# Two layers of attention and retention on one core: the last head's steps spread among the attention branch's groups, and a product's operands made by halves

## What is computed

```python
h = rms_norm(x, norm_g[layer])
z = h @ w_in[layer]
qa, ka, va, ga, qr, kr, vr, gr, gm = split_columns(z)
# attention branch: 8 query heads, 2 key heads, head dimension 64
oa = block_attention(qa, ka, va)
ya = (silu(ga) * oa) @ w_branch_attn[layer]
# retention branch: 4 heads of dimension 128, chunks of 128 tokens,
# a forward scan plus a strictly backward scan
orr = head_group_norm(bidirectional_retention(qr, kr, vr, lg_f, lg_b), ret_gn_w[layer])
yb = (silu(gr) * orr) @ w_branch_ret[layer]
# merge
gates = sigmoid(gm)
merged = gates[:, :, 0] * ya + gates[:, :, 1] * yb
x = x + merged @ w_out[layer]
```

## Time and profile before

| | |
|---|---|
| median of 3 runs | 1881.06 us (1879.89 to 1881.47) |
| the profiled execution | 1879.79 us |
| its span | 1878.0 us |
| TensorE (PE) busy | 1765.7 us, 94% |
| VectorE (DVE) busy | 1286.2 us, 68% |
| ScalarE (ACT) busy | 791.3 us, 42% |
| GpSimd (POOL) busy | 670.8 us, 36% |
| mean granted clock of TensorE | 0.985 |

### The profile page before, as it was taken

One profiled execution on the slowest core, in us unless ns is written; L12 is line 12 of the kernel. 1 busy time (PEld: TensorE's weight loads), 2 busy tenths in 40 slices (PEclk: granted clock), 3 DMA queues, 4 the chain that ended last, 5 costly groups with the idle time before them and its releaser, 6 DMA issues.

```text
span 1878.0 us, 30204 instructions
## 1 busy us (share of the span) xinstructions
PE 1765.7 (94%) x10592; PEld 1560.9 (83%) x10592; DVE 1286.2 (68%) x2658; ACT 791.3 (42%) x1759; POOL 670.8 (36%) x581
## 2 busy tenths in 40 slices
PE   5799989999999999999998998999999989999986
PEld 5688978899998788887787888889999978888865
DVE  6879678625544386769987877794445553867798
ACT  4368448622222243333344873683222222433333
POOL 0058227624323223223601761485223422232241
PEclk9999999999999999999999999999999999999998
DMA  7000000111011223224130001001011113122322
GB/s 265 23 12 12 27 23 24 36 33 46 22 36 54 102 64 105 79 95 152 45 116 23 23 1 49 12 12 46 24 45 45 45 62 118 58 89 83 131 79 90
DMA packets 136664, 113.07 MB, mean 60 GB/s; under 512 B 16480, under 2 KB 115040, under 8 KB 136544
## 3 DMA queue, kind: packets, MB, share of 16 engines
q1 hardware_dynamic: 134144, 106.20, 17.6%
q10 hardware_dynamic: 2400, 5.31, 0.8%
HBM read 90.52 MB, written 20.97 MB: 59 GB/s over the span
## 4 chain that ended last, share of the span: by engine, by line
PE 68%; DVE 20%; issue 4%; ACT 3%; POOL 2%; DMA 1%; SPq 0%; POOLq 0%; DVEq 0%; ACTq 0%
PE ps L754 16%; PE ps L756 16%; PE ps L755 16%; PE ps L890 5%; PE ps L879 4%; DVE xh L2168 3%; PE ps L903 3%; PE ps L905 3%; DVE hT_lo L2155 2%; PE ps L996 2%; DVE us L1900 2%; PE ps L980 1%; DVE pT_lo L1812 1%; DVE lsum L2146 1%; DVE nmx L1804 1%
## 5 line engine op out<-in xcount | busy, mean ns | idle before, releaser
L754 PE MATMUL ps<-w_hi,hT_hi 128*128 128x256 f32 (+1 forms) x1280 | 391.5, 306 | 13.4 <-DVE hT_lo L1658 4.8
L756 PE MATMUL ps<-w_hi,hT_lo 128*128 128x256 f32 (+1 forms) x1280 | 377.1, 295 | 0.0
L755 PE MATMUL ps<-w_lo,hT_hi 128*128 128x256 f32 (+1 forms) x1280 | 376.8, 294 | 0.0
L754 PEld LDWEIGHTS ps<-w_hi,hT_hi 128*128 128x128 f32 x1280 | 245.1, 191 | 18.5 <-DVE hT_lo L1658 7.0
L755 PEld LDWEIGHTS ps<-w_lo,hT_hi 128*128 128x128 f32 x1280 | 245.4, 192 | 0.3
L756 PEld LDWEIGHTS ps<-w_hi,hT_lo 128*128 128x128 f32 x1280 | 244.8, 191 | 0.0
L610 POOL TENSOR_SCALAR pp<-pp,rrc 128x1024 f32<-128x1024 f32 x128 | 144.0, 1125 | 167.0 <-DVE rrc L1817 160.1
L1812 DVE TENSOR_TENSOR pT_lo<-ps,pT_hi 128x512 fp32r<-128x512 f32 x256 | 164.3, 683 | 26.6 <-ACT pT_hi L1300 25.3
L556 POOL TENSOR_SCALAR w_hi<-raw 128x1024 fp32r<-128x1024 f32 x65 | 69.2, 1064 | 309.6 <-PE ps L756 272.8
L1804 DVE TENSOR_REDUCE nmx<-ps 128x1 f32<-128x1024 f32 x128 | 154.2, 1205 | 2.6 <-PE ps L879 2.6
L890 PE MATMUL ps<-idf,pp 128*128 128x128 f32 x1024 | 140.8, 278 | 15.5 <-DVE pT_lo L1812 9.1
(11 more groups left out here) (215 smaller groups left out, 4131.3 us busy)
## 6 DMA issues: line engine op xcount, KB each, us to landing
raw<-w_in SPq DMA_DIRECT2D x167, 256.0 KB, 3.3
xs<-xh SPq DMA_DIRECT2D x2, 4096.0 KB, 16.5
ys<-y_st SPq DMA_DIRECT2D x32, 256.0 KB, 2.0
hb<-ys SPq DMA_DIRECT2D x16, 512.0 KB, 4.5
xh<-xs SPq DMA_DIRECT2D x8, 1024.0 KB, 7.3
raw<-w_a SPq DMA_DIRECT2D x16, 256.0 KB, 3.1
raw<-w_r SPq DMA_DIRECT2D x16, 256.0 KB, 3.2
w<-w_o SPq DMA_DIRECT2D x4, 1024.0 KB, 6.9
```

The source lines that it names most:

```text
L754: nc.tensor.matmul(outp, ah, bh, start=(start and i == 0), stop=False)
L755: nc.tensor.matmul(outp, ah, bl, start=False, stop=False)
L756: last = nc.tensor.matmul(outp, al, bh, start=False, stop=(stop and i == len(pairs) - 1))
```

## The change

The last head's update moves behind group 0, on TensorE and on ScalarE; the scores with the states move from behind groups 0 and 1 to behind groups 2 and 3; the output turns (and ScalarE's copies of them) from behind group 4 to behind group 8. The first four groups use banks 2, 0, 1, 3 in this order, and so every four, with the waits for the masked scores at group 0 and for the gates at group 1. In the output projection VectorE makes product 1's left sum, right low part and left low part for the first half, then for the second; and GpSimd's sum for product 2 waits for six finished low parts of the left, that is until product 1's is complete.

```diff
@@ -71,6 +71,8 @@
+
+A_BANK = (2, 0, 1, 3)
@@ -728,6 +730,8 @@ (right_sum, GpSimd)
+                    if p == 2:
+                        pool.wait_ge(o_alo, L * (2 * N_P) + 6)
@@ -1054,9 +1058,9 @@ (branch, TensorE)
                             if g == 0:
+                                pe.wait_ge(c_pm, (L + 1) * (RH * T))
+                            elif g == 1:
                                 pe.wait_ge(c_g, (L + 1) * (RH * T))
-                            elif g == 2:
-                                pe.wait_ge(c_pm, (L + 1) * (RH * T))
@@ -1066,18 +1070,19 @@
-                    prod3(ps[:, 4 * br + g % 4, :],
+                    prod3(ps[:, 4 + g % 4 if br else A_BANK[g % 4], :],
...
-                update(RH - 1, T - 1)
                 for g in range(N_G):
                     branch(0, g)
-                    if g < 2:
-                        cross(RH - 1, 2 * g)
-                        cross(RH - 1, 2 * g + 1)
-                    if g == 4:
+                    if g == 0:
+                        update(RH - 1, T - 1)
+                    if 2 <= g <= 3:
+                        cross(RH - 1, 2 * g - 4)
+                        cross(RH - 1, 2 * g - 3)
+                    if g == 8:
                         turn_out(RH - 1, 0)
                         turn_out(RH - 1, 1)
@@ -1400,7 +1405,7 @@ (spill, ScalarE)
-                    nc.scalar.copy(y_st[:, g % 2], ps[:, g % 4]).then_inc(y_ev, 1)
+                    nc.scalar.copy(y_st[:, g % 2], ps[:, A_BANK[g % 4]]).then_inc(y_ev, 1)
@@ -2130,7 +2136,7 @@ (VectorE)
-                def left_sum(p):
+                def left_sum(p, halves=(0, 1)):
...
-                    for h in range(2):
+                    for h in halves:
...
@@ -2191,9 +2197,10 @@
-                left_sum(1)
-                right_lo(1)
-                left_lo(1)
+                for h in range(2):
+                    left_sum(1, (h,))
+                    right_lo(1, (h,))
+                    left_lo(1, (h,))
                 left_sum(3)
                 add_up(0)
```

More of the change, by code:

```diff
@@ L2144, in left_sum, with left_lo @@
                     (r, kr, _), (q, kq, sign) = LEFT[p]
-                    for h in range(2):
+                    for h in halves:
                         V.tensor_tensor(left_total(p, h), left(r, kr, h), left(q, kq, h),
                                         ALU.add if sign > 0 else ALU.subtract).then_inc(o_sum, 1)
-                def left_lo(p):
-                    for h in range(2):
+                def left_lo(p, halves=(0, 1)):
+                    for h in halves:
                         dve.wait_ge(o_ahi, L * (2 * N_P) + 2 * ORDER_A.index(p) + h + 1)
@@ L2168, in add_up, with right_lo @@
                             V.scalar_tensor_tensor(o, ps[:, O_BANK[p] + i, :], 0.5 * sign, o, ALU.mult, ALU.add).then_inc(o_post, 1)
-                def right_lo(p):
+                def right_lo(p, halves=(0, 1)):
                     if p == 0:
                         dve.wait_ge(o_blo, L * (2 * N_P) + 2 * N_P)
-                    for h in range(2):
+                    for h in halves:
                         dve.wait_ge(o_bhi, L * (2 * N_P) + 2 * p + h + 1)
```

## The result

The changed kernel takes 1858.85 us (median of 5 runs, 1856.85 to 1863.0). The kernel before, run beside it, has 1879.89 (1878.84 to 1881.47). The ratio is 0.9891, with a 95% interval of 0.9875 to 0.9907: 21 us less, clear of the 0.2% that a measurement can tell. The profiled execution took 1857.64 us, its span is 1855.8, 22.2 under that of before.

What follows compares the result with a forecast made beforehand. TensorE, busy 94% of the span, was taken as the bound, VectorE at the output projection's start. Gains of 18.5 (branch changeover) and 3.8 us (second product) sum to 22.3: 1881.06 - 22.3 = 1858.8 us, range 1854 to 1866.

Steps and rivals of the forecast that it cites:

- The seam: From the last retention head's last matmul to the retention branch: 48.83 us a layer for 58.1, saving 18.5 in both.
- chain: VectorE's six-step backward chain before the scores with the states: starts 1.6 us later, at 1523.65, and ends at 1528.15.
- scores: TensorE's first scores with the states, after groups 0 to 2 and the update: at 1528.8, no wait, margin 0.65 us.
- The second step: Second of the backward chain's six steps: held by GpSimd's rounding of weights until 1526.6, as the third was before.
- the turns' operand: VectorE's last product before the output turns: ready at 1546.7, 1.9 us before TensorE comes to the turns.
- The queues: Shifted work on SP, GpSimd and ScalarE around the attention groups: costs nothing, so 9.25 us reach the layer's end.
- SP's blocked spill: Group 0's spill, 1.9 us earlier, stands behind a weight load until 1526.43; ScalarE needs its buffer at about 1529.2.
- The product: Output projection's second product: one of two VectorE operations held by GpSimd is freed, 1.9 us a layer, 3.8 in all.
- the nearest pair: Output projection's two VectorE sums at 1803.69, 4.56 us with one operation held: model for product 1's sums, 4.5 us.
- my upper bound: Output projection: both collisions go, 4.4 us a layer; as a rival (or cheaper changeovers) 1854.5 us, chance 0.06.
- The clock did not fall without pauses: Rival: without pauses TensorE's clock falls to 1.2 GHz in the branch groups, up to 1936 us; chance 0.02.
- rival 1: Scores with the states still wait, 1.6 us showing: costs 3.2 us over both layers, 1862 us; chance 0.08.

Runs made afterwards that it cites:

- the two runs without the halves: Kernel before with only GpSimd's new wait for product 2's sum, 1875.53 us; changed kernel with product 1's operations in their old order, 1854.80 us.
- the wait alone: Kernel before with only GpSimd's new wait for product 2's sum, product 1's operations in their old order: 1875.53 us in one execution.
- the update alone: Kernel before with only the last update moved behind group 0, with the new banks: 1881.59 us for 1877.97 beside it, one execution each.
- the turns alone: Kernel before with only the output turns and ScalarE's copies moved from behind group 4 to behind group 8: 1873.14 us for 1877.97.
- the product alone: Kernel before with only the output projection's edits, product 1's order by halves and GpSimd's new wait: 1877.41 us, ratio 0.9985.
- the halves alone: Kernel before with only product 1's operations ordered by halves, GpSimd's sum starting when its load lands: 1880.51 us.

## Why the prediction was right

**The seam** was forecast at 48.83 us a layer and took 48.63 and 48.61 in the changed kernel, and 48.61 to 48.63 in all eight seams of the four other executions with it unaltered: the sum of its work alone. The gain forecast as 18.5 us was 18.9. Each step came where it was put, counted from the slot's end: chain from 3.75 (forecast 3.81) to 8.31 (8.31) in both layers, scores at 8.88 (8.96), turns at 28.7 (28.8), GpSimd's fifth unit 8.0 us earlier (8). The second step is the long one where it was looked for: it took 2.45 of the chain's 4.56 us, and a free one takes 0.35. Off was the turns' operand, which I had ready 1.9 us early with all old stalls counted in; it was 4.7 us early, for GpSimd's rounding now falls beside VectorE's reads of the accumulators and holds nothing (the first product with the gate takes 0.69 us for 2.75).

**The queues** were not quite free. I gave SP's blocked spill a margin for group 2 and there was none: ScalarE's third copy waited 4.31 us for the transfer and began at 1520.38, 2.2 us after its group. It was hidden, because group 6 is the first that needs it. The step "all this costs nothing" stands; the reason given for that spill does not.

**The product** was forecast at 1.9 us a layer from the nearest pair, and 2.0 came, by the mechanism named: two held operations became one. But its parts were misread. The halves add nothing, and the wait without them shortens the lead-in by 4.36 us: my upper bound, both collisions gone, was the true value there, and I gave it 0.06. That 1.9 fits the edit as made is the work of the pair chosen as a model, not of an understanding of who gets in when. Nor is a shorter lead-in always a shorter layer: it was in layer 1, and in layer 0 of the two runs without the halves nearly all of it was lost again behind the lead-in. The Trainium skill, SBUF — State Buffer, section Who interferes with whom, states the exclusion, and that the order of issue decides who waits. The trace agrees on both for the operation that runs when GpSimd is released: in the pairs shown it is not the one held. About the operations behind it the section says nothing, and there both outcomes occur: with the same 0.25 us between the starts GpSimd got in after one operation in the changed kernel and only after both without the halves. The outcome was the same in both layers, and in a second kernel with this output projection. What decides it was not found. At product 1 the order of VectorE's operations ahead of the pair turns it; at product 3, with the wait alone, that order is the old one and the pair is free all the same, so the order is not the whole answer.

**The rivals.** The scores did not wait, with 0.57 us to spare for the forecast 0.65; one group earlier they do. The clock did not fall without pauses: 1.00 over the whole seam. The price of rival 1, though, was set by "idle times of 1.04 and 1.64 us left the clock alone"; 2.03 us did it once and not the other time, and in three other runs the clock fell behind the turns, whose idle times are 1.64 and 1.10 us (last section). So a wait of 1.6 us there would have had to be priced with and without 1.7 us more.

**The sum.** 1858.8 against 1858.85 is closer than the terms are, and that is luck. 22.3 was forecast and 22.9 came in the four stages, but a stage untouched by the change gave 0.9 back in the profiled execution. And the forecast was taken from a median of 1881.06, while the kernel before has 1879.89 beside the changed one, so by medians the gain was 21.0. The runs of the changed kernel spread over 6 us.

## What to carry to other kernels

Price a chain of waits as a chain: here the update alone (with the new banks) cost 0.4 us in one layer and 1.6 in the other, the turns alone gave 3.2, and the three moves together gave 9.4, all that stood idle. When work is put in front of a wait, take the group sum without waits as the target, then check each step's inputs against it in turn, and look for a buffer whose last reader is done (here 1.5 to 1.9 us). When two engines exclude each other, place the one off the path beside operations that don't collide, and follow the push to the sum behind it and to the end of the layer: a stage that got shorter is not yet a shorter kernel.

## What the runs showed of the hardware

An idle time of TensorE does not fix what the clock does. After 2.03 us the granted clock was 1.00 in one layer and 0.65 in the other of one execution. Four kernels have the old seam and ran at full clock: the kernel before, the product alone, the wait alone and the halves alone. Their idle times agree: about 2.7 us (layer 0) or 3.1 (layer 1) before the first scores, 1.6 to 1.8 and 1.1 before the turns. In the run with the halves alone, layer 0, the clock did not fall at all, neither behind the scores nor behind the turns; in layer 1 it fell at both places. The windows start at the scores and at the second turn of each layer:

```profile
609.54:613.54 4.00, 4.00 (x18) 3.43 (x19) 2.59 (x8) 0.00 (x0) 0.00 (x0) 1.00 0.59 190
627.55:631.55 4.00, 4.00 (x20) 3.37 (x21) 1.36 (x2) 1.23 (x2) 0.00 (x0) 1.00 0.26 75
1526.80:1530.80 4.00, 4.00 (x11) 3.26 (x12) 1.72 (x5) 0.00 (x0) 0.00 (x0) 0.61 0.58 186
1546.38:1550.38 4.00, 4.00 (x13) 3.22 (x14) 1.36 (x2) 0.69 (x1) 0.00 (x0) 0.58 0.21 64
```

In layer 0 of the run with the product alone it held behind the scores and fell behind the turns:

```profile
610.91:614.91 4.00, 4.00 (x18) 3.41 (x19) 2.59 (x8) 0.00 (x0) 0.00 (x0) 1.00 0.58 187
628.95:632.95 4.00, 4.00 (x14) 3.23 (x15) 1.36 (x2) 0.69 (x1) 0.00 (x0) 0.62 0.23 68
```

The old seam took 56.4 us where the clock did not fall, 58.0 to 58.2 where it fell once and 59.6 to 59.7 where it fell twice, so a fall costs about 1.6 us. The old seam thus varies by up to 3 us a layer, and the changed one by 0.02.

The other finding is that of the port. GpSimd's operation, released 0.22 to 0.26 us after VectorE had begun a run of two-input operations, waited for one of them in some kernels. In others it waited for the whole run: with the wait alone one such operation lasted 9.15 us, for 2.4 free. At product 1 the outcome was the same in both layers, and in all kernels with the same output projection, so the program fixes it there and not the execution.
